# Picked tokens fetched by row number from memory instead of gathered by one-hot products

## The reference, cut to what matters

```python
def expert_choice_ffn(h, w_router, w_gate, w_up, w_down):
    bsz, n_tok, d = h.shape
    cap = EC_CAPACITY_FACTOR * n_tok // N_EXPERTS
    aff = jax.nn.softmax((h @ w_router).astype(jnp.float32), axis=-1)
    gate, idx = lax.top_k(jnp.swapaxes(aff, 1, 2), cap)
    xg = jax.vmap(lambda hb, ib: hb[ib])(h, idx)
    a = jnp.einsum('becd,edf->becf', xg, w_gate)
    u = jnp.einsum('becd,edf->becf', xg, w_up)
    y = jnp.einsum('becf,efd->becd', jax.nn.silu(a) * u, w_down) * gate[..., None].astype(h.dtype)
    return jax.vmap(lambda yb, ib: jnp.zeros((n_tok, d), h.dtype).at[ib.reshape(-1)].add(
        yb.reshape(-1, d)))(y, idx)
```

## Time and profile before

| | |
|---|---|
| median of 3 runs | 3190.81 us (3184.38 to 3193.99) |
| the profiled execution's own time | 3193.39 us |
| its span on the core | 3191.6 us |
| TensorE busy (matmuls) | 2995.6 us, 94% of the span |
| DVE, ACT, POOL busy | 1876.5, 1357.6, 546.3 us |
| mean granted TensorE clock | 0.951 of full |
| DMA | 580.80 MB, mean 182 GB/s |
| chain of work that ended last | PE 76%, DVE 8%, DMA 7%, issue 3%, ACT 2% |

### The profile page before, as it was taken

One profiled execution on the slowest core, in us unless ns is written; L12 is line 12 of the kernel. 1 busy time (PEld: TensorE's weight loads), 2 busy tenths in 40 slices (PEclk: granted clock), 3 DMA queues, 4 the chain that ended last, 5 costly groups with the idle time before them and its releaser, 6 DMA issues.

```text
span 3191.6 us, 42921 instructions
## 1 busy us (share of the span) xinstructions
PE 2995.6 (94%) x17920; PEld 2461.0 (77%) x17920; DVE 1876.5 (59%) x2079; ACT 1357.6 (43%) x1751; POOL 546.3 (17%) x218
## 2 busy tenths in 40 slices
PE   4999989999997999999989998899999799999998
PEld 2979877999896676767659798899999766676765
DVE  4542644324316989888865427341351488989897
ACT  2133230111106767777741432310110577777775
POOL 2413213233211000000024133152332100000000
PEclk7989899999988999999989898799998799999999
DMA  8523447557514989898985234332443198989896
GB/s 232 73 34 60 87 113 198 131 161 172 136 70 147 345 285 343 279 346 282 344 225 75 32 64 83 73 67 40 80 80 113 55 348 296 327 296 329 300 324 235
DMA packets 357650, 580.80 MB, mean 182 GB/s; under 512 B 13712, under 2 KB 148880, under 8 KB 357328
## 3 DMA queue, kind: packets, MB, share of 16 engines
q1 hardware_dynamic: 297488, 501.26, 53.8%
q10 hardware_dynamic: 51808, 56.53, 5.6%
q0 software_dynamic: 8160, 20.26, 2.0%
HBM read 568.54 MB, written 9.45 MB: 181 GB/s over the span
## 4 chain that ended last, share of the span: by engine, by line
PE 76%; DVE 8%; DMA 7%; issue 3%; ACT 2%; DVEq 2%; SPq 1%; ACTq 0%; POOL 0%; POOLq 0%
PE ps L826 27%; PE ps L1310 8%; PE ps L1313 8%; PE ps L1318 8%; PE ps L792 5%; DMA ring<-w_down 3%; PE ps L1227 2%; DVE w_lo L2242 2%; PE ps L868 2%; PE ps L1088 2%; DVEq L1969 2%; DMA ring<-w_gate 1%; PE ps L900 1%; ACT w_hi L1440 1%; PE ps L1005 1%
## 5 line engine op out<-in xcount | busy, mean ns | idle before, releaser
L2242 DVE TENSOR_TENSOR w_lo<-ring,w_hi 128x2048 fp32r<-128x2048 f32 x256 | 584.3, 2287 | 99.3 <-ACT w_hi L1440 98.6
L826 PE MATMUL ps<-h_hi,w_hi 128*128 128x320 f32 x1792 | 560.2, 313 | 3.7 <-DVE arena L2020 2.0
L826 PE MATMUL ps<-h_lo,w_hi 128*128 128x320 f32 x1792 | 555.6, 310 | 0.0
L826 PE MATMUL ps<-h_hi,w_lo 128*128 128x320 f32 x1792 | 555.6, 310 | 0.0
L1440 ACT ACTIVATE w_hi<-ring 128x2048 fp32r<-128x2048 f32 x256 | 486.6, 1909 | 82.7 <-DMA ring<-w_up 24.5
L671 POOL CAST w_hi<-ring 128x2048 fp32r<-128x2048 f32 (+1 forms) x76 | 143.0, 1881 | 1607.0 <-DMA ring<-w_in 1007.6
L1500 ACT ACTIVATE arena<-ps,par 128x640 f32<-128x640 f32 x88 | 70.0, 796 | 705.3 <-PE ps L826 675.7
L673 POOL TENSOR_TENSOR w_lo<-ring,w_hi 128x2048 fp32r<-128x2048 f32 (+1 forms) x76 | 345.7, 4548 | 29.3 <-issue 28.5
L826 PEld LDWEIGHTS ps<-h_hi,w_hi 128*128 128x128 f32 x1792 | 338.4, 189 | 6.3 <-issue 3.9
L826 PEld LDWEIGHTS ps<-h_lo,w_hi 128*128 128x128 f32 x1792 | 338.2, 189 | 0.5 <-issue 0.5
L826 PEld LDWEIGHTS ps<-h_hi,w_lo 128*128 128x128 f32 x1792 | 338.0, 189 | 0.0
(11 more groups left out here) (311 smaller groups left out, 5472.5 us busy)
## 6 DMA issues: line engine op xcount, KB each, us to landing
ring<-w_gate SPq DMA_DIRECT2D x128, 1024.0 KB, 5.8
ring<-w_up SPq DMA_DIRECT2D x128, 1024.0 KB, 6.2
ring<-w_down SPq DMA_DIRECT2D x128, 1024.0 KB, 6.9
ring<-w_in SPq DMA_DIRECT2D x64, 1024.0 KB, 13.1
arena<-ada_w ACTq DMA_DIRECT2D x40, 1024.0 KB, 6.2
arena<-ada_w SPq DMA_DIRECT2D x8, 1024.0 KB, 15.5
arena<-biasT ACTq DMA_DIRECT2D x16, 512.0 KB, 6.0
ring<-w_o SPq DMA_DIRECT2D x8, 1024.0 KB, 14.6
```

The costliest lines, as they stand in the source:

```text
L826: last = pe.matmul(ps[:, bank(u) + half, 0:HALF], w[:, k, f0:f0 + P], a[:, k, at], start=(k == 0 and part == 0), stop=(k == KD - 1 and par ...
L2242: dve.tensor_tensor(w_los[g % NW], ring[:, s, :], w_his[g % NW].bitcast(F32), ALU.subtract).then_inc(slot_used[s], 1)
```

## The change

The tokens are kept once, in full (`h_tok`), and written to a new tensor in memory, `tok_dram` (640 rows of 1024 numbers). For each expert the 80 numbers of the picked tokens are computed, and one indirect DMA on POOL's queue fetches these rows to `xg_tok`, 80 partitions by 1024 numbers. TensorE turns them by plain transposes, four of 80 columns for each feature tile, into the same PSUM banks. The number of a token comes out of `gate_cols`: `aff` has a 17th column that holds the token's number, and each narrow product has two columns, gate and number. So `gate_cols` now has to run before the fetch: behind `picks` for the first quad, and behind chunk 2 of the quad before's last expert for the others, with `picks` moved on DVE from behind chunk 3 to behind chunk 1, and DVE's copy of the numbers (`picked_cols`) behind chunk 4.

```diff
-        tok_hi = sb("tok_hi", [P, NTILE, D], F32R)
-        tok_lo = sb("tok_lo", [P, NTILE, D], F32R)
+        h_tok = sb("h_tok", [P, NTILE, D])
+        xg_tok = sb("xg_tok", [P, 4, D])
+        tok_idx = sb("tok_idx", [P, 4], mybir.dt.uint32)
...
@@ POOL, after a layer's last weight split
                 for t in range(NTILE):
                     pool.wait_ge(*tok_copied.at(l, 2 * t + 2))
-                    pool.tensor_tensor(tok_lo[:, t, :], h_tok[:, t, :], tok_hi[:, t, :].bitcast(F32),
-                                       ALU.subtract).then_inc(tok_low.sem, 1)
+                    pool.dma_start(tok_dram[t * P:(t + 1) * P, :], h_tok[:, t, :]).then_inc(tok_stored.sem, 16)
+                pool.wait_ge(*tok_stored.at(l, NTILE))
+                for quad in range(NQUAD):
+                    pool.wait_ge(*gate_col_ready.at(l, quad + 1))
+                    if quad:
+                        pool.wait_ge(*gather_ps.at(l, KD * quad))
+                    pool.sem_inc(pool_passed, 1)
+                    for i in range(4):
+                        pool.indirect_dma_start(xg_tok[0:CAP, i, :], None, tok_dram[:, :],
+                                                bass.IndirectOffsetOnAxis(tok_idx[0:CAP, i:i + 1], 0))\
+                            .then_inc(tok_landed.sem, 16)
...
@@ PE, gather
                 if dt == 0:
-                    pe.wait_ge(*pick_ready.at(l, quad + 1))
-                    if quad:
-                        pe.wait_ge(*scat_ready.at(l, 3 * quad))
+                    pe.wait_ge(*tok_landed.at(l, 4 * quad + 4))
+                    pe.wait_ge(*gate_col_ready.at(l, quad + 1))
...
-                for t in range(1, NTILE):
-                    for part, tok in enumerate((tok_hi, tok_lo)):
-                        pe.matmul(out[:, :, 0:CAP_S], tok[:, t, at], pick_s[:, t - 1, :, :],
-                                  start=(t == 1 and part == 0), stop=(t == NTILE - 1 and part == 1))
-                for part, tok in enumerate((tok_hi, tok_lo)):
-                    last = pe.matmul(out[:, :, CAP_S:CAP], tok[:, 0, at], pick_p[:, :, 0:CAP_P],
-                                     start=(part == 0), stop=(part == 1))
+                for i in range(4):
+                    last = pe.transpose(ps[:, GATHER_BANK[dt], i * CAP:(i + 1) * CAP],
+                                        xg_tok[0:CAP, i, dt * P:(dt + 1) * P], ident[0:CAP, 0:CAP])
                 last.then_inc(gather_ps.sem, 1)
...
@@ PE, gate_cols
-                pe.wait_ge(*xg_ready.at(l, KD * quad + 7))
+                pe.wait_ge(*pick_ready.at(l, quad + 1))
+                if quad:
+                    pe.wait_ge(*scat_ready.at(l, 3 * quad))
...
@@ PE, expert and the layer's start
-                    if i == 0 and c == 0:
-                        gate_cols(l, quad)
+                    if i == 3 and e < NE - 1 and c == 2:
+                        gate_cols(l, quad + 1)
...
-                pe.wait_ge(*tok_low.at(l, NTILE))
+                gate_cols(l, 0)
                 for dt in range(KD):
                     gather(l, 0, dt)
...
@@ ACT, the tokens by rows
-                    act.activation(tok_hi[:, t, at], ps[:, n % 4, :], ACT.Copy, scale=rcol[:, t:t + 1])
                     act.activation(h_tok[:, t, at], ps[:, n % 4, :], ACT.Copy, scale=rcol[:, t:t + 1])
...
@@ DVE
+            def picked_cols(l, quad):
+
+                dve.wait_ge(*gate_ps.at(l, quad + 1))
+                if quad:
+                    dve.wait_ge(*tok_landed.at(l, 4 * quad))
+                src = ps[0:CAP, 2, 0:8].rearrange("p (i a) -> p a i", a=2)
+                dve.tensor_copy(gate_col[0:CAP, quad % 2, :], src[:, 0, :])
+                dve.tensor_copy(tok_idx[0:CAP, :], src[:, 1, :]).then_inc(gate_col_ready.sem, 1)
...
-                    if i == 0 and c == 2:
-                        dve.wait_ge(*gate_ps.at(l, quad + 1))
-                        dve.tensor_copy(gate_col[0:CAP, :], ps[0:CAP, 2, 0:4]).then_inc(gate_col_ready.sem, 1)
+                    if i == 3 and e < NE - 1 and c == 4:
+                        picked_cols(l, quad + 1)
...
-                    if i == 3 and e < NE - 1 and c == 3:
+                    if i == 3 and e < NE - 1 and c == 1:
                         picks(l, quad + 1)
```

More of the change, by code:

```diff
@@ L63 @@
 K_ID, K_ONE, K_BLK, K_ROT, K_COS, K_SIN = 0, 128, 256, 384, 512, 1024
-K_TRI, K_IOTA, K_SEL = 1536, 1792, 1856
-NCONST = 1858
+K_TRI, K_IOTA, K_TOK = 1536, 1792, 1856
+NCONST = K_TOK + T // 128
 NSLOT = 4
@@ L315, in step_program @@
         y_p = ff(128, D)
[L316 to L320, removed]
+        aff_tok = ff(1152, NTILE, NE + 1)
+        aff = aff_tok[:, :, 0:NE]
+        posT = ff(1240, NTILE, NE)
+        smax = ff(1320, NTILE)
+        gate_col = ff(1328, 2, 4)
         zeros = view(FF_AT - 3200, T)
@@ L440, in step_program @@
         posT_ready = signal("posT_ready", 1)
-        tok_low = signal("tok_low", NTILE)
+        tok_stored = signal("tok_stored", NTILE, 16)
+        tok_landed = signal("tok_landed", 4 * NQUAD, 16)
         pick_ready = signal("pick_ready", NQUAD)
@@ L1222, in gather @@
                     pe.wait_ge(*xg_ready.at(l, KD * quad + reused[dt] + 1))
-                out = ps[:, GATHER_BANK[dt], 0:4 * CAP].rearrange("p (e c) -> p e c", e=4)
-                at = slice(dt * P, (dt + 1) * P)
-                for t in range(1, NTILE):
-                    for part, tok in enumerate((tok_hi, tok_lo)):
-                        pe.matmul(out[:, :, 0:CAP_S], tok[:, t, at], pick_s[:, t - 1, :, :],
-                                  start=(t == 1 and part == 0), stop=(t == NTILE - 1 and part == 1))
-                for part, tok in enumerate((tok_hi, tok_lo)):
-                    last = pe.matmul(out[:, :, CAP_S:CAP], tok[:, 0, at], pick_p[:, :, 0:CAP_P],
-                                     start=(part == 0), stop=(part == 1))
+                for i in range(4):
+                    last = pe.transpose(ps[:, GATHER_BANK[dt], i * CAP:(i + 1) * CAP],
+                                        xg_tok[0:CAP, i, dt * P:(dt + 1) * P], ident[0:CAP, 0:CAP])
                 last.then_inc(gather_ps.sem, 1)
             def gate_cols(l, quad):
-                pe.wait_ge(*xg_ready.at(l, KD * quad + 7))
+                pe.wait_ge(*pick_ready.at(l, quad + 1))
+                if quad:
+                    pe.wait_ge(*scat_ready.at(l, 3 * quad))
                 for i in range(4):
                     e = 4 * quad + i
+                    at = slice(2 * i, 2 * i + 2)
+                    two = slice(e, NE + 1, NE - e)
                     for t in range(1, NTILE):
-                        pe.matmul(ps[0:CAP_S, 2, i:i + 1], pick_s[:, t - 1, i, :].bitcast(F32), aff[:, t, e:e + 1],
+                        pe.matmul(ps[0:CAP_S, 2, at], pick_s[:, t - 1, i, :].bitcast(F32), aff_tok[:, t, two],
                                   start=(t == 1), stop=(t == NTILE - 1))
-                    last = pe.matmul(ps[CAP_S:CAP, 2, i:i + 1], pick_p[:, i, 0:CAP_P].bitcast(F32), aff[:, 0, e:e + 1],
+                    last = pe.matmul(ps[CAP_S:CAP, 2, at], pick_p[:, i, 0:CAP_P].bitcast(F32), aff_tok[:, 0, two],
                                      start=True, stop=True)
@@ L2150, in route @@
                 dve.memset(zeros[0:NE, :], 0.0)
+                dve.tensor_copy(aff_tok[:, :, NE], cst[:, K_TOK:K_TOK + NTILE])
                 dve.memset(y_p, 0.0)
@@ L2267, in expert @@
                         dve.scalar_tensor_tensor(act_row[0:CAP, half, :], ps[0:CAP, 4 + 2 * half, :],
-                                                 gate_col[0:CAP, i:i + 1], silu_t[0:CAP, :], ALU.mult, ALU.mult)\
+                                                 gate_col[0:CAP, quad % 2, i:i + 1], silu_t[0:CAP, :], ALU.mult, ALU.mult)\
                             .then_inc(act_ready.sem, 1)
@@ L2367, in _ @@
                 picks(l, 0)
+                picked_cols(l, 0)
                 for dt in range(KD):
@@ L2405, in constants @@
     k[:, K_IOTA:K_IOTA + CAP_S] = 1 + np.arange(CAP_S)
-    k[:, K_SEL:K_SEL + 2] = np.arange(P)[:, None] % 32 == np.arange(2)[None, :]
+    k[:, K_TOK:K_TOK + NTILE] = P * np.arange(NTILE)[None, :] + np.arange(P)[:, None]
     return k
@@ L2467 @@
     aps.append(nc.dram_tensor("x_copy", (P, KD, T), mybir.dt.float32, kind="Internal").ap())
+    aps.append(nc.dram_tensor("tok_copy", (T, D), mybir.dt.float32, kind="Internal").ap())
     step_program(nc, *aps)
```

3 lines of the change are left out of this document (1 added, 2 removed).

## The result

The changed kernel took 3246.72 us (median of 4 runs, 3240.42 to 3250.05), beside 3188.51 for the kernel before on the same chip: ratio 1.0181 (95% interval 1.0155 to 1.0207), 58 us slower. The forecast was 3199.4 with a range that ended at 3226: the sign of its sum was right, its size was not.

A forecast was written before the change was run, and what follows sets the result against it. TensorE was taken as never idle, with ACT also full in the gather. Two layer starts at +11.6 us and six later quads at -3 gave +8.6 on 3190.8, so 3199.4 us, range 3182 to 3226.

The forecast's parts named there:

- the sign of its sum: Whole kernel: terms 11.6 - 3 summed to +8.6 us, slower than the kernel before.
- Later quads without the fetch: Six later quads, fetch costed at nothing: +0.3 or -1.4 us a quad, middle -0.5 taken, -3 for six.
- 3.8 and 0.4: Later quads: 3.8 us gained by chunk 1 starting earlier, 0.4 by a wait at the gather that should go.
- between 2.75 and 4.5: Later quads: `gate_cols` ahead of ACT's chain costs 2.75 us, plus 1.75 if the clock is not saved at the old place.
- The clock: TensorE's lower clock behind `gate_cols` costs 1.75 us ahead of ACT's chain; at the old place 1.75 are saved or none.
- +0.3 and not its middle: Later quads' sum: +0.3 us a quad without the clock saving, -1.4 if the clock holds; middle -0.5 taken.
- Later quads, the fetch: Later quads: the fetch's 1.31 MB cost nothing, engines being free a tenth of 160 us; without cover 3.5 us a quad.
- the third rival: Last expert's chunks: the fetch meets full-rate loads and DMA becomes the bound, 21 us more, 3221; chance 0.12.
- A layer's start: First quad of a layer: `gate_cols` 4.5 us, fetch 8 (4.7 to 11.3) in series; chunk 2 +5.8 us later, +11.6 for two.
- Off the path: Ranking time: five 512 KB stores, 7 us of DMA, fit while DMA is idle; with the removed copies and subtractions, costed at nothing.
- The slow-fetch rival: POOL's queue ahead of each quad: slow indirect loads, 3220 at 4 us a fetch, 3321 at 7; chance 0.10.
- the two fetch terms: The fetch in later quads, costed at nothing, and at a layer's start, taken as 8 us.

The follow-up runs named there:

- E1: Changed kernel without the 24 indirect loads of the later quads (first quad's rows read again): ratio 1.0085 to the kernel before, six quads 954 us.
- E5: Changed kernel without the later quads' indirect loads and without 19 of each later quad's 20 narrow products: ratio 0.9991 to the kernel before, six quads 935 us.
- E4: Changed kernel with POOL instead of ACT making the high part of each gathered tile: ratio 1.0068 to the kernel before, six quads 954 us.
- E8: Kernel before with POOL instead of ACT making the high part of each gathered tile: ratio 1.0003, six quads 959 us.
- E9: Changed kernel with numbers made a quad ahead, fetch sent once they are there, low parts ahead of gathered tiles at starts: ratio 1.0029 to the kernel before.
- E3: Changed kernel without 19 of the 20 narrow products of each later quad; fetch kept: ratio 1.0087 to the kernel before, six quads 968 us.
- E12: E11 with DVE's first low part at a start held until the fetch landed, the others behind the gathered tiles: ratio 0.9939 to the kernel before.
- E11: E9 plus POOL making the high parts and DVE's low parts at a start behind the first fetch's issue: ratio 0.9943 to the kernel before.
- E10: Changed kernel with DVE's three low parts at a start ahead of the gathered tiles, waiting for the first fetch's issue: ratio 1.0175 to the kernel before.
- E7: Changed kernel with numbers a quad ahead, fetch in the third expert, low parts first at starts, POOL making high parts: ratio 1.0036 to the kernel before.
- E2: Changed kernel with a plain load of 80 fixed rows instead of each indirect load: ratio 1.0137 to the kernel before, six quads 972 us.

## Why the prediction was wrong

**Later quads without the fetch: right, the number in part by luck.** The forecast was -0.5 us a quad; E1 measures -0.4 ((954 - 956.2) / 6). With fetch and numbers gone (E5) a quad gains 3.5 us, where the prediction had 3.8 and 0.4; the narrow products then take 3.1 back, where it had between 2.75 and 4.5. That ACT's chain and not TensorE sets chunk 1 in the changed kernel is shown by E4, and E8 shows that before, without TensorE's relief, it did not. The clock is not saved at the old place in five of the six quads: chunk 1 still takes 4.2 to 4.4 us behind its wait. By the prediction's own sum that gives +0.3 and not its middle; the products cost less than it had, the gain was smaller too, and with the middle taken for the clock the misses nearly cancel.

**Later quads, the fetch: the step that failed.** "The engines are free for a tenth of 160 us, so I cost it at nothing; without that cover it is 3.5 us a quad." The cover is not where the fetch is. The kernel before shows it, from the start of a quad's last expert to the end of its chunk 8's matmuls, in the gather behind them, and in the next quad's first expert (the last but one figure of a row is the DMA engines' share):

```profile
1111.00:1137.00 26.00, 25.71 (x114) 16.22 (x112) 23.93 (x16) 19.54 (x15) 0.00 (x0) 1.00 0.97 341
1137.00:1155.00 18.00, 17.87 (x120) 15.01 (x120) 11.42 (x13) 15.97 (x26) 0.00 (x0) 1.00 0.77 273
1155.00:1192.00 37.00, 36.97 (x197) 25.67 (x196) 32.41 (x33) 22.51 (x22) 0.00 (x0) 0.95 0.70 240
```

The tenth is free in the second and third of these stretches; the fetch lies almost wholly in the first, where the share is 0.97. E1 prices the fetch at 4.8 us a quad, 29 us in all, and by E9 fetch and products together cost 1.1 in other places. The 3.5 was low as well, since a fetched row takes the engines longer than weights do: 5.2 us for a quad's rows. This was the third rival in mechanism, to which I had given 0.12 and 21 us. My argument against it, that the narrow products delay TensorE by 4.5 us just there, was wrong: by E3 and E5 this delay gives the loads only some 0.7 us a quad (the products cost 3.1 without the fetch and 2.4 with it).

**A layer's start: right order, one term too small.** Forecast +5.8, measured +10.3 and +10.2. `gate_cols` takes 4.4 (forecast 4.5), and from the rows to chunk 2 it is 16.0 (forecast 15.6, from 1000.1 to 1015.7). The fetch takes 12.4, from 997.37 to 1009.78, where I took 8 between 4.7 and 11.3: that is the whole miss. Three parts of it were not in my bounds: POOL's 0.9 us between signal and first issue, 1.2 and not 0.7 from one issue to the next, and a first issue of 2.13. Counted from the first issue, the first layer's fetch lands in 9.05 us by itself (E12), in 11.5 in the changed kernel with one low part and its load beside it, and in 12.3 and 14.1 with more low parts and the loads that they set free (E11, E10). So its surroundings cost 2.5 us, and even alone it takes 10 with POOL's 0.9, above my middle.

**Off the path: right.** The five stores took 0.53 to 0.59 us to issue and landed in 2.9 to 3.5 while tokens were ranked; nothing waited for them.

**The slow-fetch rival did not happen.** An issue for 80 rows takes 0.89 us alone. The Trainium skill (GPSIMD Engine Reference, Performance pitfalls for Q7 kernels), from which the prediction worked out an estimated 6.8 us a fetch, does not fit this kind of load; the trace decides.

Sum of the terms as measured: 20.5 + 26.7 = 47 us (forecast 11.6 - 3 = 8.6), of which the two fetch terms are missed by 29 and 9; and the remaining 9 to 11 of the 58 lie in stretches that the change doesn't touch. Why they were longer in the changed kernel's runs is open.

## What to carry to other kernels

Before a transfer is called covered, look at the DMA share of the very stretch into which it falls and at whether loads are ahead there; a mean over a cycle hides that the free part and the full part are different places. Where two engines are full together, work taken from one is worth what the other allows, and the second engine's relief (E4, E11) is what turns the first one's into time. A new serial chain at a start is priced by its hand-overs, and by what other engines do beside it.

## What was not expected of the hardware

POOL's indirect issue stands still when it begins while DVE makes a low part, which reads two tensors in SBUF. E7 shows it best: its third issue met two low parts back to back.

```profile
1005.97 2.28 DVE L2267 TENSOR_TENSOR w_lo<-ring,w_hi 128x2048 fp32r<-128x2048 f32 x1
1008.17 2.28 DVE L2267 TENSOR_TENSOR w_third<-ring,w_third 128x2048 fp32r<-128x2048 f32 x1
```

```profile
1005.06 0.93 POOL L769 DMA_INDIRECT xg_tok<-tok_copy,tok_idx  x1 [0.30 <-issue]
1006.29 4.93 POOL L769 DMA_INDIRECT xg_tok<-tok_copy,tok_idx  x1 [0.30 <-issue]
1011.52 0.89 POOL L769 DMA_INDIRECT xg_tok<-tok_copy,tok_idx  x1 [0.30 <-issue]
```

4.93 us, of which 4.16 lie beside the two low parts. In all runs together 161 indirect issues began clear of a low part and took 0.88 to 0.99 us, also 38 in which a low part began after the issue had (at 1263.63 in E7, 0.89 us with 0.83 beside one). The 132 that began 0.1 us or more into a low part took 1.86 to 4.94 us: 122 of them ended 0.76 to 0.85 us after that low part did, and 10, as here, were held by a second one straight behind it. Why some are held twice and others are not (1.88 us at 1010.59 in E12, 0.76 of it beside the second) is open. Plain loads on the same queue took 0.51 to 0.55 everywhere (E2). The Trainium skill (SBUF — State Buffer, Who interferes with whom) says that a DVE instruction with two SBUF inputs contends with a POOL instruction that reads SBUF, and not with one that only writes it. The trace agrees with both halves, if an indirect issue reads its row numbers and a plain one has none to read; that this is the reason was not tried by itself.
